# Two modulation vectors computed on VectorE from transposed weights, in place of small TensorE products

## The reference, cut to what matters

```python
silu_c = jax.nn.silu(c)            # c: (1, 1024), for the 512 tokens
silu_cc = jax.nn.silu(c_ctx)       # c_ctx: (1024,), for 256 context tokens
for l in range(DEPTH):             # DEPTH = 2
    mx = jnp.split((silu_c @ w_mod[l] + b_mod[l])[:, None, :], N_MOD, axis=-1)
    mc = jnp.split(silu_cc @ w_mod[l] + b_mod[l], N_MOD, axis=-1)
```

## Time and profile before

| what | value |
|---|---|
| median of 3 runs | 3601.41 us (3600.73 to 3603.17) |
| the profiled execution's own time | 3601.05 us |
| span of the profiled execution | 3599.3 us |
| PE busy | 3520.0 us, 98% |
| DVE busy | 1715.6 us, 48% |
| ACT busy | 1386.0 us, 39% |
| mean granted clock of TensorE | 0.996 |

### The profile page before, as it was taken

The page is one execution under the profiler, slowest core; times in us unless marked ns, Lnnn a source line. Parts: engine busy times, 40 slices in busy tenths (PEclk is TensorE's granted clock), DMA queues, the critical chain, the costliest instruction groups (busy, mean ns, idle before and its releaser), DMA issues.

```text
span 3599.3 us, 47276 instructions
## 1 busy us (share of the span) xinstructions
PE 3520.0 (98%) x17985; PEld 2669.0 (74%) x17985; DVE 1715.6 (48%) x2500; ACT 1386.0 (39%) x2058; POOL 3.4 (0%) x11
## 2 busy tenths in 40 slices
PE   8999999999999999999999899999999999999999
PEld 5666787777776667887777764488888885369998
DVE  6675434434466754344334456543323355643334
ACT  5554323222255543233222334532322334443334
POOL 0000000000000000000000000000000000000000
PEclk9999999999999999999999999999999999999999
DMA  4222233555532222345655210022222221023332
GB/s 129 57 60 59 83 95 109 147 151 152 151 92 57 60 59 84 95 124 147 173 156 147 69 44 4 7 59 65 64 60 63 64 79 56 4 59 91 91 93 88
DMA packets 576335, 310.35 MB, mean 86 GB/s; under 512 B 28400, under 2 KB 567104, under 8 KB 576192
## 3 DMA queue, kind: packets, MB, share of 16 engines
q1 hardware_dynamic: 575792, 308.18, 30.5%
q10 hardware_dynamic: 400, 0.20, 0.0%
HBM read 297.32 MB, written 2.10 MB: 83 GB/s over the span
## 4 chain that ended last, share of the span: by engine, by line
PE 93%; DVE 3%; ACT 2%; issue 1%; DMA 1%; SPq 0%; DVEq 0%; ACTq 0%
PE ps L1109 14%; PE ps L1110 14%; PE ps L1111 14%; PE ps L1423 10%; PE ps L1425 10%; PE ps L1427 10%; PE ps L1611 2%; PE ps L1593 2%; PE ps L1309 2%; PE ps L1272 1%; PE ps L1193 1%; PE ps L1288 1%; PE ps L1552 1%; PE ps L1306 1%; PE ps L1278 1%
## 5 line engine op out<-in xcount | busy, mean ns | idle before, releaser
L1775 ACT ACTIVATE whi<-wraw 128x1024 fp32r<-128x1024 f32 x448 | 470.7, 1051 | 549.1 <-DMA wraw<-in_w_mlp 246.6
L1109 PE MATMUL ps<-uhi,whi 128*128 128x512 f32 (+1 forms) x1456 | 610.2, 419 | 11.6 <-DVE wlo L2417 4.8
L2417 DVE TENSOR_TENSOR wlo<-wraw,whi 128x1024 fp32r<-128x1024 f32 x448 | 545.9, 1219 | 106.6 <-ACT whi L1775 102.1
L1111 PE MATMUL ps<-uhi,wlo 128*128 128x512 f32 (+1 forms) x1456 | 571.7, 393 | 0.0
L1110 PE MATMUL ps<-ulo,whi 128*128 128x512 f32 (+1 forms) x1456 | 571.7, 393 | 0.0
L1109 PEld LDWEIGHTS ps<-uhi,whi 128*128 128x128 f32 x1456 | 273.7, 188 | 100.7 <-issue 35.8
L1110 PEld LDWEIGHTS ps<-ulo,whi 128*128 128x128 f32 x1456 | 273.9, 188 | 71.1 <-issue 14.8
L1111 PEld LDWEIGHTS ps<-uhi,wlo 128*128 128x128 f32 x1456 | 273.3, 188 | 65.1
L1423 PE MATMUL ps<-u2hi,whi 128*128 128x512 f32 (+1 forms) x1216 | 295.5, 320 | 3.3 <-DVE wlo L2417 2.4
L1423 PE MATMUL ps<-yhi,whi 128*128 128x512 f32 (+1 forms) x976 | 295.7, 353 | 0.0
L1427 PE MATMUL ps<-yhi,wlo 128*128 128x512 f32 (+1 forms) x976 | 295.1, 353 | 0.0
(11 more groups left out here) (327 smaller groups left out, 4555.6 us busy)
## 6 DMA issues: line engine op xcount, KB each, us to landing
wraw<-in_w_in SPq DMA_DIRECT2D x128, 512.0 KB, 3.8
wraw<-in_w_mlp SPq DMA_DIRECT2D x128, 512.0 KB, 4.0
mod_raw<-in_w_mod SPq DMA_DIRECT2D x96, 512.0 KB, 5.4
wraw<-in_w_mlp_in SPq DMA_DIRECT2D x64, 512.0 KB, 4.4
wraw<-in_w_mlp_out SPq DMA_DIRECT2D x64, 512.0 KB, 3.8
wraw<-in_w_branch SPq DMA_DIRECT2D x16, 512.0 KB, 3.3
wraw<-in_w_out SPq DMA_DIRECT2D x16, 512.0 KB, 3.7
wraw<-in_w_o SPq DMA_DIRECT2D x16, 512.0 KB, 3.8
```

Of the source, the lines that this page charges most:

```text
L1109: pe.matmul(bank, whs[:, i], x_hi[:, k], start=(i == 0), stop=False)
L1111: last = pe.matmul(bank, wls[:, i], x_hi[:, k], start=False, stop=(i == n - 1))
L1775: act.activation(whi[:, r], wraw[:, r], ACT.Copy).then_inc(w_hi, 1)
L2417: dve.tensor_tensor(wlo[:, r], wraw[:, r], whi[:, r].bitcast(F32), ALU.subtract).then_inc(w_split, 1)
```

## The change

The weights are handed over transposed (`w_mod` as outputs x inputs), and the conditions replicated on all 128 partitions. Outputs then lie on partitions from the start: for a block of 128 outputs and one condition, one `tensor_tensor_reduce` on DVE multiplies 128x1024 weights with the 128x1024 replicated vector and sums along the row into one column of `mod_part`. The product itself goes to two PSUM banks as scratch. Three blocks x two conditions make six such operations a group; `MOD_TURNS` puts one, two, two and one behind the steps b = 0 to 3. PE's products and transposes, DVE's copies and sums over parts, and their semaphores go. In each first-stack layer the silu of the replicated conditions (two 128x1024 sigmoids on ACT, two products on DVE) is made within the output projection, behind its seventh chunk, in the memory of the gates. The memory plan shifts with it, so three of the four static weights of the second stack load later (`late_weights`), and PE waits for them only before their first use. Waits are added: PE's `wide_norm` for the last sum of layer 1, DVE's MLP of layer 1 for `context_kept`.

```diff
+MOD_TURNS = (((0, 0),), ((0, 1), (1, 0)), ((1, 1), (2, 0)), ((2, 1),))
...
-        silu = sb("silu", [P, KT, 2])
-        silu_parts = sb("silu_parts", [P, KT, 32])
+        mod_part = sb("mod_part", [P, MOD_GROUP, 2])
...
+        silu = gates[:, :, :].rearrange("p (v half) c -> p v (half c)", v=2)
...
-                                    sp.wait_ge(mod_made, made + (l * MOD_COLS + MOD_GROUP * KT // RAW * half + n))
-                                    sp.dma_start(mod_raw[:, n - 1], w_mod[:, :, bass.ds(c, P)])\
-                                      .then_inc(mod_in[n - 1], 16)
+                                    group = 2 * KT // RAW * q + i + KT // RAW * half
+                                    sp.wait_ge(mod_summed, 2 * MOD_GROUP * group + (2 * MOD_COLS * l + 2 * n))
+                                    sp.dma_start(mod_raw[:, n - 1], w_mod[bass.ds(c, P), :]).then_inc(mod_in[n - 1], 16)
...
+                    if j == RAW:
+                        sp.wait_ge(v_ready, s.heads_split_end)
+                        sp.dma_start(silu[:, :, :], a["conditions"]).then_inc(conditions_in, 16)
...
+            sp.wait_ge(mod_summed, 2 * MOD_COLS * DEPTH + 2 * MOD_GROUP)
+            late_weights(0)
...
-            def mod_product(b, group):
-
-                pe.wait_ge(mod_in[b], 16 * group + 16)
-                pe.wait_ge(mod_kept, MOD_GROUP * group + (b + 1))
-                for half in range(2):
-                    for lane in range(4):
-                        k = 4 * half + lane
-                        last = pe.matmul(ps[32 * lane:32 * (lane + 1), SCORE + b, 0:P], silu_parts[:, k, :],
-                                         mod_raw[:, b, k], start=(half == 0), stop=(half == 1))
-                last.then_inc(mod_made, 1)
-
-            def mod_turn(group):
...
                 if s is plan.layers[-1]:
+                    pe.wait_ge(silu_ready, s.layer + 1)
                     turn_context()
-
-                pe.wait_ge(silu_ready, 1)
...
                 if s.layer == 0:
+                    pe.wait_ge(mod_summed, 2 * MOD_COLS * DEPTH + 2 * MOD_GROUP)
                     wide_norm(s.norm1)
...
+                    if step is late:
+                        pe.wait_ge(late_in, 48 * (s.layer + 1))
...
                 for j in range(KT):
                     tile = s.out.tile + j
+                    if j == KT - 2:
+                        act.wait_ge(conditions_in, 16 * s.layer + 16)
+                        for v in range(2):
+                            half = ps[:, SCORE + 2 * v:SCORE + 2 * v + 2, :].rearrange("p b c -> p (b c)")
+                            sigmoid(half, silu[:, v]).then_inc(silu_sig_ready, 1)
+                        exp_and_log()
...
+            def silu_of_conditions(l):
+
+                for v in range(2):
+                    dve.wait_ge(silu_sig_ready, 2 * l + v + 1)
+                    half = ps[:, SCORE + 2 * v:SCORE + 2 * v + 2, :].rearrange("p b c -> p (b c)")
+                    last = dve.tensor_tensor(silu[:, v], silu[:, v], half, ALU.mult)
+                last.then_inc(silu_ready, 1)
+                dve.wait_ge(silu_ready, l + 1)
...
                 for j in range(KT):
+                    if j == KT - 1:
+                        silu_of_conditions(l)
                     lo_before(s.out.chunk + j)
...
                     made = 2 * KT // RAW * QUARTERS * l + group
-                    if b == RAW - 2:
-                        for c in range(MOD_GROUP):
-                            dve.wait_ge(mod_made, MOD_GROUP * made + (c + 1 + MOD_GROUP))
-                            dve.tensor_copy(mod_rows[:, P * c:P * (c + 1)], ps[:, SCORE + c, 0:P]).then_inc(mod_kept, 1)
-                    elif b == RAW - 1:
-                        dve.wait_ge(mod_turned, made + 1)
-                        parts = ps[:, ATT, 0:MOD_GROUP * P].rearrange("p (c s x) -> p c x s", c=MOD_GROUP, x=32)
-                        dve.tensor_reduce(mod[:, l, bass.ds(MOD_GROUP * group, MOD_GROUP), :], parts[:, :, 0:2, :],
-                                          axis=AX.X, op=ALU.add)
+                    if b == 0:
+                        dve.wait_ge(mod_kept, made + 1)
+                    for c, v in MOD_TURNS[b]:
+                        dve.wait_ge(mod_summed, 2 * MOD_GROUP * made + (2 * MOD_GROUP + 2 * c + v - 1))
+                        if v == 0:
+                            dve.wait_ge(mod_in[c], 16 * made + 16)
+                        scratch = ps[:, SCORE + 2 * v:SCORE + 2 * v + 2, :].rearrange("p b c -> p (b c)")
+                        dve.tensor_tensor_reduce(scratch, mod_raw[:, c],
+                                                 silu[:, v], 1.0, 0.0, ALU.mult, ALU.add,
+                                                 mod_part[:, c, v:v + 1]).then_inc(mod_summed, 1)
+                    if b == RAW - 1:
+                        dve.wait_ge(mod_summed, 2 * MOD_GROUP * made + 4 * MOD_GROUP)
+                        dve.tensor_copy(mod[:, l, bass.ds(MOD_GROUP * group, MOD_GROUP), :], mod_part[:, :, :])                            .then_inc(mod_kept, 1)
...
                 inverse_root(s.norm2.root)
+                if s is plan.layers[-1]:
+                    dve.wait_ge(context_kept, 4)
```

More of the change, by code:

```diff
@@ L1470, in _ @@
                 if s.layer == 0:
+                    pe.wait_ge(mod_summed, 2 * MOD_COLS * DEPTH + 2 * MOD_GROUP)
                     wide_norm(s.norm1)
-                pe.wait_ge(static_in, 64 * (s.layer + 1) + 16)
+                pe.wait_ge(static_in, 16 * (s.layer + 1) + 16)
+                late = next(step for step in s.mixer if step.name in ("fourier_map", "values", "head_key", "conv_map"))
                 pe.wait_ge(second_const, 2)
@@ L3080 @@
         ("diff_q_norm", 0), ("diff_k_norm", 0), ("gqa_q_norm", 2), ("gqa_k_norm", 2))], axis=1)}
[L3081 removed]
+    conditions = np.stack([inputs["c_2"].reshape(-1), inputs["c_ctx_2"].reshape(-1)])
+    rows = {"conditions": np.broadcast_to(conditions, (P, *conditions.shape))}
+    for name, value in {**inputs, **constants(), **gains, **rows}.items():
+        if name == "w_mod_2":
+            value = np.swapaxes(value, 1, 2)
         if name == "w_in":
```

61 lines of the change are left out of this document (17 added, 44 removed).

## The result

| | us |
|---|---|
| before, median of the runs | 3601.4 (3600.7 to 3603.2) |
| changed kernel, median of the runs | 3513.9 (3511.8 to 3516.5) |
| ratio, 95% interval | 0.9755 (0.9743 to 0.9768) |
| predicted | 3556 (3540 to 3585) |
| profiled execution after; its span | 3511.8; 3510.0 |

It is also more than all the work that was taken off PE, 63.0 us. So something beside the modulation became faster. The page of the changed kernel: busy time of the engines, the clock that TensorE was granted in 40 slices, the chain that ended last, and two of its groups.

What follows compares the result with a forecast made beforehand. PE was taken to bound the kernel (93% of the last chain). -57.1 + 2.1 + 1.0 + 5.6 + 2.8 = -45.6 us took the profiled 3601.05 to 3555.4, its median to 3556 us, range 3540 to 3585.

Steps and rivals of the forecast that it cites:

- PE brings a chunk every 5.60: MLP groups: a PE chunk without extra work stays at 5.60 us, so groups of four chunks take 22.4 us.
- What the change removes: Section counting modulation work taken off PE: 63.0 us in 32 groups, of which 57.1 us counted as gain.
- The price of an operation: Each multiply-and-sum on DVE takes 1.4 us, between 1.22 and 1.8.
- 29 groups at 1.97 us: MLP groups where PE sets the pace each lose 1.97 us of modulation; -57.1 us.
- Silu, +2.1 and +1.0: Output projections: silu work makes PE wait, +2.1 us for layer 0's MLP `wlo`, +1.0 us before layer 1's context turn.
- The turn between the layers, +5.6: Layer 0 to layer 1: added DVE operations delay the normed halves PE awaits, +5.6 us; that group's products gain nothing.
- The end of layer 1, +2.8: Last eight down steps: DVE never makes up its lag, the norm's product starts 2.8 us later, last two groups included.
- Half rate: Rival: the DVE operation takes two steps per element, 2.47 us each; total 3656 us, slower; chance 0.10.
- A large fixed cost: Rival: each DVE operation costs 1.8 us, so the gain is 26 us; total 3575 us; chance 0.14.
- the ends are hidden: Rival: something else limits the layer turn and end, so only silu costs; total 3541 us; chance 0.13.
- weight loads slip behind SP's wait: Rival that nothing moves: SP's new wait delays weight loads until PE waits for them; about 3600 us; chance 0.03.
- The last sentence of the prediction: Sign of being wrong: an operation over 1.6 us, or PE's chunk spacing in plain quarters above 5.60.

Runs made afterwards that it cites:

- a_pad32: Changed kernel with 32 unused bytes behind mod_part, restoring the earlier operand distance; 3554.8 us, ratio to before 0.9869.
- b_far224: Kernel before, modulation still on TensorE, with 224 unused bytes behind silu_parts, timed in rounds; 3563.8 us, ratio 0.9899.
- a_order: Changed kernel with the first multiply-and-sum of a turn moved between the addition and the sum of squares in down halves; 3507.5 us, ratio to before 0.9743.

## Why the prediction was wrong

The step that failed is the one in which PE's time for a chunk was carried over as it was: "PE brings a chunk every 5.60", and groups of four at 22.4 us. It is 5.44 us in the changed kernel, with each product 6.6 ns shorter. The prediction gives no reason why it should stay, and has no term for it: "What the change removes" and "What it adds" count instructions, DMAs and waits. The two tensors that go and the one that comes were read in the diff for what they hold, not for what stands behind them. The sum lacks a term of about -40 us: `a_pad32` to the changed kernel is -40.9, and before to `b_far224` is -37 with the old modulation. The two parts by themselves add up to 47 + 37 = 84 us, 3.5 less than both together (5.5 by the traces). Of the traces' 5.5, 2.8 lie in the first 60 us and 1.5 behind 624.95 in `a_pad32`: stretches of 3 to 7 us at the clock's 1.2 GHz level which the changed kernel's trace doesn't have, or has shorter. Could it have been foreseen? Not its size: all long products of before run at one distance, and no row shows another. But the question could have been asked, since the diff shows two allocations fewer ahead of all moving operands, and a range of a prediction that rests on "nothing else moves" is too narrow when addresses do move. "The change" even says that the memory plan shifts; only the later loads were drawn from it.

The rest is told by `a_pad32`, in which the term is taken out. **Its 3554.8 us stand against the predicted 3556.** The mechanisms of the sum were right, but that the total agrees so closely is partly luck: two terms were 4.8 us too large together, and the clock, which has no term, cost 2.9 us. Its PE timeline at the places of the steps:

```profile
624.54 0.53 PE L1119 MATMUL ps<-uhi,whi 128*128 128x512 f32 x1 [2.04 <-DVE wlo L2403]
...
985.86 0.70 PE L1388 MATMUL ps<-root,mats 128*128 128x256 f32 x2 [1.58 <-DVE root L2459]
991.26 0.36 PE L1119 MATMUL ps<-uhi,whi 128*128 128x256 f32 x1 [1.91 <-DVE ulo L2470]
...
1590.01 1.97 PE L1188 MATMUL ps<-ident,crow 128*128 128x128 f32 x16 [0.78 <-DVE gates L2395]
...
1960.08 2.93 PE L1419 MATMUL ps<-root,mats 128*128 128x512 f32 x4 [6.24 <-DVE mod_part L2669]
```

- *The price of an operation.* Taken: 1.4 us. Measured: 1.24 us, and from the start of one to the start of the next 1.18 (718.52 to 719.70 in the first timeline, where the read of the sum already overlaps), a little under even the low bound of 1.22. The estimate erred by adding the small instruction's whole time.
- *29 groups at 1.97 us.* In the plain quarters no step of PE is longer than before by more than 0.35 us, and chunks take 5.60 us: right.
- *Silu, +2.1 and +1.0.* PE's step there grows from 0.23 to 2.43 us (+2.2) and from 0.23 to 1.17 (+0.9): right. The wait for `wlo` was named.
- *The turn between the layers, +5.6.* PE steps that grew: 1.75, 2.07 and 1.31 us, less 0.5 twice, +4.1. Smaller, as the operation is cheaper. And the products of the last group were held to gain nothing, but the step of PE that held them (1007.75 before) shrank by 1.5 us, as in every other group. So the turn costs 2.6 us, not 5.6. For layer 0 as a whole -29.6 + 2.1 + 5.6 = -21.9 was predicted (15 groups), -22.9 measured. The two are closer than their parts, since TensorE's clock took 1.5 us back behind the wait at 624.54 (granted 0.50 from 624.95 to 628.20, the first row of the next fence; the kernel before has 1.00 there).
- *The end of layer 1, +2.8, with the last two groups in it.* The norm's wait grew from 2.31 us to 6.24, 0.8 stands ahead of the last chunks; against it stand the products of the last two groups, which went too. Up to the norm's start layer 1 gains 25.6 us, where -27.6 + 1.0 + 2.8 = -23.8 was predicted, so the end costs 1.0 us, not 2.8. That DVE never makes up its lag there is what the timeline shows. Then the norm's four products, 1.56 us before, took 2.93: PE had stood still since 1953.9, and its granted clock fell to 0.50 from 1956.2 on (second row). With the 1.4 us lost by it, -24.2 is measured for the whole layer.

```profile
core 0: us, PE busy (x) PEld busy (x) DVE busy (x) ACT busy (x) POOL busy (x), PEclk, DMA share, GB/s
624.95:628.20 3.25, 3.25 (x9) 2.55 (x8) 1.48 (x3) 2.19 (x3) 0.00 (x0) 0.50 0.78 271
1956.20:1973.10 16.90, 7.57 (x19) 5.17 (x20) 12.54 (x22) 7.60 (x12) 1.56 (x2) 0.50 0.31 94
```

- *The rivals.* Half rate is out: 1024 elements in 1.24 us are the rate of the plain pass of the earlier trace rows. This operation with two SBUF float32 sources, its product going to PSUM, isn't slowed. The Trainium skill, "Vector Engine (DVE) Microarchitecture Reference", section "Points that are easy to get wrong", has the halving for `S2S2D2_STT` with two non-bf16 SBUF sources. The prediction counted the multiply-and-sum among that family; the trace lists it as CUSTOM_DVE_ANT_0, so it shows the halving to be absent here, not whether the rule is meant for it. A large fixed cost is out with it. That the ends are hidden is out too: `a_order` gains 4.3 us from the wait at the end alone. That weight loads slip behind SP's wait until PE waits for them is not seen: plain chunks keep their 5.60 us.
- *The last sentence of the prediction* named a chunk spacing above 5.60 us as what would prove it wrong, and never one below.

## What to carry to other kernels

Removing or resizing a tensor moves all that is allocated behind it, and can change the time of instructions that nobody touched; when a change to buffers gains or loses more than it should, look first whether the step of an untouched product changed, and lay the two traces' matmuls side by side. Compare at equal places (a pad of unused bytes restores them), or two effects get one name. And work that fits beside the bound in a steady stretch shows up at the ends, where nothing is left to catch up in: put it into the waits there, or some steps earlier.

## What the runs showed of the hardware

- A float32r product of 512 columns steps by 226.7 ns when the moving operand stands a multiple of 256 bytes behind both weight tensors, and by 229 to 234 ns otherwise, at nearly the same granted clock (0.993 to 0.996 in the kernels of the table): 6720 such products in the first stack x 6.6 ns = 44 us at most, of which the heads hide a part. Moving weights and operands together changes nothing there. The Trainium skill, "SBUF — State Buffer", section "Operand start alignment", treats an operand's start as a matter of legality and says that its runs timed nothing; these runs show no cost of a start either, but one of the distance between two operands.
- Where 512 and 256 columns alternate, as with `yhi` and `ylo` in the second stack, distances 0 and 32 are alike (512 columns 231.2 and 228.3 ns, the 256 behind them 115.4 and 118.3), and 64, 96 and 128 are slower (353.3, 350.1 and 351.1 for the two together, where 0 and 32 have 346.6).
- After PE had stood still for some 2 us at the end of layer 1 (1953.9 to 1956.2 in `a_pad32`), and after its wait of 2.04 us at 624.54, the granted clock was 0.50 for 17.1 and 3.4 us; the products in these stretches cost 1.4 and 1.5 us more. Not every wait did this: the changed kernel's PE waited 2.36 us for the same `wlo` (613.68), and its clock stayed at 1.00.
- The multiply-and-sum over 128x1024 float32 with a PSUM destination for the product: 1.24 us, and 0.14 for the read of the sum, which hides behind the next instruction unless that one waits for it.
- Rows of 4 KB land in 3.6 us where pieces of 512 bytes took 5.4; it wasn't on the path in either kernel.
